# Layer attention with maxima two steps ahead, ends of heads spread over steps, and low parts on VectorE

## The reference

```python
hn = rmsnorm(h, norm_gain[l])
dq, dk, dv, dg, fq, fk, fv, ff, fg = split(hn @ w_in[l])
# differential attention: 4 heads of 2 maps, keys 64 wide, values 128 wide
s = einsum('bhmqd,bhmkd->bhmqk', q, k) * HEAD_DIM ** -0.5      # chunk-wise causal mask
p = softmax(s)
do = einsum('bhqk,bhkd->bhqd', p[:, :, 0] - lam * p[:, :, 1], v)
do = rmsnorm(do, subln_gain[l], 1e-5) * (1.0 - lam_init) * silu(dg)
# forgetting attention: 8 heads, keys and values 64 wide
s = einsum('bhqd,bhkd->bhqk', q, k) * HEAD_DIM ** -0.5 + cq[..., None] - cum_logf[:, :, None, :]
fo = einsum('bhqk,bhkd->bhqd', softmax(s), v) * silu(fg)       # causal mask
h = h + concatenate([do, fo], -1) @ w_out[l]
```

## Time and profile before

| | us |
|---|---|
| median of 3 runs | 1854.41 |
| lowest and highest | 1851.5, 1854.45 |
| the profiled execution | 1854.35 |
| its span | 1852.5 |
| attention of layer 0 | 196 to 331 in the span |
| attention of layer 1 | 551 to 677 in the span |

### The profile page before, as it was taken

One profiled execution on the slowest core, in us unless ns is written; L12 is line 12 of the kernel. 1 busy time (PEld: TensorE's weight loads), 2 busy tenths in 40 slices (PEclk: granted clock), 3 DMA queues, 4 the chain that ended last, 5 costly groups with the idle time before them and its releaser, 6 DMA issues.

```text
span 1852.5 us, 29994 instructions
## 1 busy us (share of the span) xinstructions
PE 1807.5 (98%) x11996; PEld 1630.0 (88%) x11996; DVE 1202.5 (65%) x1687; ACT 815.1 (44%) x1475; POOL 517.5 (28%) x437
## 2 busy tenths in 40 slices
PE   9999999999998899999999999999999999999999
PEld 8999888989988887999988877989877879999887
DVE  7843475575526757999985555646666589999531
ACT  5222466332235754444433324446565554444331
POOL 3443333344342433000034423320133410000343
PEclk9999999999999999999999999999999999999999
DMA  4333120223331112332323223200003223323223
GB/s 167 97 96 109 54 48 24 80 89 101 98 108 42 36 46 91 121 126 96 103 74 98 96 98 126 83 34 1 1 1 114 91 65 118 126 92 103 73 98 103
DMA packets 46170, 154.16 MB, mean 83 GB/s; under 512 B 6096, under 2 KB 6352, under 8 KB 45904
## 3 DMA queue, kind: packets, MB, share of 16 engines
q1 hardware_dynamic: 46032, 152.24, 25.2%
HBM read 140.40 MB, written 2.10 MB: 77 GB/s over the span
## 4 chain that ended last, share of the span: by engine, by line
PE 87%; DVE 7%; ACT 3%; issue 1%; DMA 1%; POOL 0%; SPq 0%; DVEq 0%; ACTq 0%
PE ps L476 23%; PE ps L477 23%; PE ps L478 23%; PE ps L1236 5%; PE ps L1197 4%; PE ps L1218 3%; PE ps L2895 1%; DVE nm L1285 1%; PE ps L2881 1%; PE ps L2864 1%; DVE xl L568 1%; PE ps L2634 1%; PE ps L1437 1%; DMA raw<-wstream 1%; ACT PT L1267 0%
## 5 line engine op out<-in xcount | busy, mean ns | idle before, releaser
L460 POOL TENSOR_TENSOR wl<-raw,wh 128x1024 fp32r<-128x1024 f32 (+1 forms) x166 | 407.2, 2453 | 998.8 <-ACT wh L452 998.8
L452 ACT ACTIVATE wh<-raw 128x1024 fp32r<-128x1024 f32 (+1 forms) x178 | 188.9, 1061 | 547.2 <-PE ps L478 480.8
L476 PE MATMUL ps<-xh,wh 128*128 128x264 f32 (+1 forms) x1120 | 380.0, 339 | 2.6 <-POOL wl L460 1.3
L477 PE MATMUL ps<-xl,wh 128*128 128x264 f32 (+1 forms) x1120 | 375.4, 335 | 0.0
L478 PE MATMUL ps<-xh,wl 128*128 128x264 f32 (+1 forms) x1120 | 374.8, 335 | 0.0
L478 PE MATMUL ps<-XSh,wl 128*128 128x256 f32 (+1 forms) x864 | 283.4, 328 | 0.0
L476 PE MATMUL ps<-XSh,wh 128*128 128x256 f32 (+1 forms) x864 | 283.0, 328 | 0.3 <-DVE wl L1970 0.3
L477 PE MATMUL ps<-XSl,wh 128*128 128x256 f32 (+1 forms) x864 | 283.2, 328 | 0.0
L476 PEld LDWEIGHTS ps<-xh,wh 128*128 128x128 f32 x1120 | 210.5, 188 | 29.6 <-issue 6.9
L477 PEld LDWEIGHTS ps<-xl,wh 128*128 128x128 f32 x1120 | 210.7, 188 | 22.9 <-issue 1.2
L478 PEld LDWEIGHTS ps<-xh,wl 128*128 128x128 f32 x1120 | 210.7, 188 | 22.4
(11 more groups left out here) (451 smaller groups left out, 3648.7 us busy)
## 6 DMA issues: line engine op xcount, KB each, us to landing
raw<-wstream SPq DMA_DIRECT2D x176, 512.0 KB, 3.4
rawx<-wpairs SPq DMA_DIRECT2D x44, 512.0 KB, 3.5
raw<-wpairs SPq DMA_DIRECT2D x24, 512.0 KB, 3.5
raw<-wstream SPq DMA_DIRECT2D x10, 528.0 KB, 3.4
xs<-KA SPq DMA_DIRECT2D x32, 132.0 KB, 2.4
xs<-KB SPq DMA_DIRECT2D x28, 132.0 KB, 2.3
h<-xT SPq DMA_DIRECT2D x4, 528.0 KB, 6.3
out<-h SPq DMA_DIRECT2D x8, 256.0 KB, 4.5
```

Of the source, the lines that this page charges most:

```text
L452: e.activation(wh[p % 2][:, 0:n], raw[c % 2][:, 0:n], ACT.Copy).then_inc(*w_hi(p))
L460: e.tensor_tensor(wl[p % 2][:, 0:n], raw[c % 2][:, 0:n], wh[p % 2][:, 0:n].bitcast(F32), ALU.subtract).then_inc(*w_lo(p))
L476: e.matmul(o, w_h, x_h, start=start, stop=False)
L477: e.matmul(o, w_h, x_l, start=False, stop=False)
```

## The change

It has these parts, all of them in the attention of the two layers, but for the first lines of the last two points:

- On VectorE a unit's maximum is taken at step u-2 if its scores began three steps ahead, else at u-1; the ends of heads come ahead of the maxima within a step.
- Copy and square of a differential head's end are in separate steps. The scaling is folded: in place of a reciprocal and three multiplications by it, one operation makes 128e-5 s0^2 from the sum s0 of the exponentials, which is added to the sum of squares; the copy stays unscaled.
- Ends of fox heads are one step later on VectorE.
- The quads' copies from PSUM go from VectorE to ScalarE.
- The low parts of the heads' outputs go from GpSimd to VectorE, and so do the splits of the first two chunks of `w_out`, now at steps 50 and 54.
- The last values of the meta tokens come first; at step 6 the value block comes ahead of the scores.
- The attention of the meta tokens begins at steps 14 and 25 in place of 26 and 41, in bank 0 in place of 3, and the table of banks and shut stretches follows. The last four heads' tiles are taken in the order 3, 0, 1, 2.
- The first blocks of the output projection stand at steps 61 to 66, in banks 2 and 3.

```diff
-V_SPLIT = {...} | {("wout", l, 2) for l in range(2)}
+V_SPLIT = {...} | {("wout", l, c) for l in range(2) for c in range(3)}
...
-        VALUES_PE = {-2: [(1, 0)], -1: [(2, 0), (0, 0)], 1: [(1, 1)], 2: [(2, 1)], 3: [(0, 1)], 4: [(3, 0)], 5: [(3, 1)],
-                     7: [(4, 0)], 8: [(4, 1)]}
-        VALUES_ACT, VALUES_DVE = {3: (1,), 6: (3,)}, {4: (2, 0), 9: (4,)}
+        VALUES_PE = {-2: [(1, 0)], -1: [(0, 0), (2, 0)], 1: [(0, 1)], 2: [(1, 1)], 3: [(2, 1)], 4: [(3, 0)], 6: [(3, 1)],
+                     8: [(4, 0), (4, 1)]}
+        VALUES_ACT, VALUES_DVE = {3: (1,), 7: (3,)}, {2: (0,), 4: (2,), 9: (4,)}
...
-                            self.items[q], self.on_dve[q] = x.quad[0], True
+                            self.items[q], self.on_dve[q] = x.quad[0], False
... attention_pe
+                if plan.layer is not None and s == 6:
+                    last_values_pe(e, on, plan.layer, s)
                 begin_pe(e, on, plan, s)
-                if plan.layer is not None:
+                if plan.layer is not None and s != 6:
                     last_values_pe(e, on, plan.layer, s)
...
-                if rest and s in (64, 65, 66, 67, 68, 69):
+                if plan.layer is not None and 61 <= s < 67:
                     next(rest)
... attention_dve
-                alone = plan.layer is not None and s + 1 < len(units) and units[s + 1].ahead == 1
-                if s + 1 < len(units) and not alone:
-                    maximum(s + 1)
+                layer = plan.layer is not None
+                if layer:
+                    for key, k in plan.ends.get(s, []):
+                        end_dve(e, on, plan, key, k)
+                for u in (s + 1, s + 2):
+                    if u < len(units) and u - s == (2 if layer and units[u].ahead == 3 and u > 2 else 1):
+                        maximum(u)
...
+                    if s in (50, 54):
+                        split_lo_dve(e, on, PART["wout", plan.layer, s // 4 - 12])
+                else:
+                    for key, k in plan.ends.get(s, []):
+                        end_dve(e, on, plan, key, k)
... attention_pool
-                if s in (49, 53) and plan.layer is not None:
-                    split_lo(e, on, PART["wout", plan.layer, s // 4 - 12])
...
-            return x_lo[("ao",) + key]
+            return (v_lo if key[0] in ("diff", "fox") else x_lo)[("ao",) + key]
... end_dve
             if (kind, k) in (("diff", 6), ("fox", 3)):
-                return
+                return end_low(e, on, key, v_lo)
...
+                if k == 0 and i >= 0:
+                    on.wait_ge(*prob[plan.name, last_unit[key][1]])
+                    s0 = rs[:, i % 2, 0:8:2]
+                    e.scalar_tensor_tensor(q0, s0, 128e-5, s0, ALU.mult, ALU.mult).then_inc(*v_end(*key, "q0"))
+                elif k == 3:
                     on.wait_ge(*a_end[key + ("sq",)])
...
+                    if i >= 0:
+                        on.wait_ge(*v_end.now())
+                        e.tensor_tensor(ms, ms, q0, ALU.add).then_inc(*v_end(*key, "ms"))
... layer_plan
-                shut += [(3, 26, 32), (4, 36, 37), (3, 41, 47), (4, 48, 49)]
+                shut += [(0, 14, 21), (4, 24, 25), (0, 25, 32), (4, 32, 33)]
...
-                for kind, step in (("diff", 26), ("fox", 41)):
+                for kind, step in (("diff", 14), ("fox", 25)):
... wout_begin_pe
-            next_pair(0)
-            claim(on, pair(("wout", l, 0)), wout_shape(l)[2], v_out["wout", l, 0])
-            for k in (0, 1, 2, 4, 5, 6):
-                wout_blocks(e, on, l, 0, (k,))
-                yield k
+            for c, ks in ((0, (0, 1, 2, 4, 5, 6)), (1, (0, 1, 2))):
+                next_pair(2 - 2 * c)
+                claim(on, pair(("wout", l, c)), wout_shape(l)[2], v_out["wout", l, c])
+                for k in ks:
+                    wout_blocks(e, on, l, c, (k,))
+                    yield k
+            next_pair(4)
```

More of the change, by code:

```diff
@@ L71 @@
 PARTS = list(PART)
-V_SPLIT = {(st + part, f) for st in ("ffn1", "ffn2") for part in "gu" for f in range(2, PLAIN)} | {("wout", l, 2) for l in range(2)}
+V_SPLIT = {(st + part, f) for st in ("ffn1", "ffn2") for part in "gu" for f in range(2, PLAIN)} | {("wout", l, c) for l in range(2) for c in range(3)}
 V_SPLIT |= {("ffn2u", 0), ("ffn2g", 1)}
@@ L1112, in __init__ @@
                 self.name, self.units, self.sets, self.PT, self.flip_banks = name, units, sets, PT, flip_banks
-                self.free, self.layer, self.aside = free, layer, set()
+                self.free, self.layer, self.aside, self.rest = free, layer, set(), ()
                 n, nxt = len(units), 0
@@ L1201, in attention_pe @@
             units, name = plan.units, plan.name
-            rest = None
             if plan.layer is not None:
                 last_values_pe(e, on, plan.layer, -2)
-                rest = wout_begin_pe(e, on, plan.layer)
+                plan.rest = rest = wout_begin_pe(e, on, plan.layer)
             begin_pe(e, on, plan, -1)
@@ L1299, in attention_dve @@
                         e.tensor_copy(plan.PT[i % 2][:, 0:n], PS[:, lo:lo + n]).then_inc(*v_flip(name, u))
-                if alone:
-                    maximum(s + 1)
-                if plan.layer is not None:
+                if layer:
                     last_values_dve(e, on, plan.layer, s)
@@ L1319, in attention_dve @@
                             key_low_dve(e, on, plan.layer, *head)
-                for key, k in plan.ends.get(s, []):
-                    end_dve(e, on, plan, key, k)
+                    if s in (50, 54):
[3 more added lines that the diff above has]
+                        end_dve(e, on, plan, key, k)
         def meta_values_pool(e, on, l):
@@ L1447, in end_act @@
                 compressed_act(e, on, key[1], k)
-            elif key[0] == "diff" and k == 0:
+            elif key[0] == "diff" and k in (1, 2):
                 _, _, i, nq, _ = head_shape(key)
@@ L1456, in end_act @@
                 to = fin[0:nq, f, 0:512]
-                if before:
-                    on.wait_ge(*x_hi[("ao",) + before])
-                    on.wait_ge(*ao_lo(before))
-                e.activation(to, src, ACT.Copy).then_inc(*a_end(*key, "copy"))
+                if k == 1:
+                    if before:
+                        on.wait_ge(*x_hi[("ao",) + before])
+                        on.wait_ge(*ao_lo(before))
+                    e.activation(to, src, ACT.Copy).then_inc(*a_end(*key, "copy"))
+                    return
                 on.wait_ge(*a_end[key + ("copy",)])
                 e.activation(osb[0:nq, f, 0:512], to, ACT.Square).then_inc(*a_end(*key, "sq"))
-            elif key[0] == "diff" and k == 2:
+            elif key[0] == "diff" and k == 3:
                 _, _, i, nq, _ = head_shape(key)
@@ L1534, in end_dve @@
                 d, o = osb[0:nq, f, 0:w], PS[0:nq, 512 * b:512 * b + w]
+                k -= kind == "fox"
                 if k == 0:
@@ L1574, in end_pool @@
                     end_pool(e, on, plan, (key[1], key[2], -1), k - 5)
-            elif (key[0], k) in (("mem", 2), ("nsa1", 5), ("diff", 6), ("fox", 3)):
+            elif (key[0], k) in (("mem", 2), ("nsa1", 5)):
                 end_low(e, on, key, x_lo)
@@ L1688, in layer_plan @@
             if l == 0:
-                ends[3:3], ends[6:6] = [("diff", -1)], [("fox", -1)]
+                ends[1:1], ends[4:4] = [("diff", -1)], [("fox", -1)]
             for kind, i in ends:
@@ L1694, in layer_plan @@
             heads = [[("fox", c, i, q) for i in two_] for c in range(4) for q in range(2)
-                     for two_ in ((0, 1), (2, 3))]
+                     for two_ in (((3, 0), (1, 2)) if c == 3 and q else ((0, 1), (2, 3)))]
             pairs = maps[:4] + heads[:2] + [x for pair_ in zip(maps[4:], heads[2:-2]) for x in pair_] + heads[-2:]
@@ L1771, in wout_blocks @@
             on.wait_ge(*w_hi[p])
[L1772 removed]
+            on.wait_ge(*low_part(p))
             for k in ks:
@@ L1792, in wout_pe @@
             end_pe(e, on, plans[l], *plans[l].held)
-            claim(on, pair(("wout", l, 1)), halves, v_out["wout", l, 1])
-            wout_blocks(e, on, l, 1, (0, 1, 2))
+            for _ in plans[l].rest:
+                pass
             wout_blocks(e, on, l, 0, (3, 7), True).then_inc(*tile("wout", l, 0))
@@ L3242, in gpsimd @@
                 attention_pool(e, on, plans[l])
-                parts_pool(e, on, ("wout", l, 1), ("wout", l, 7))
+                for q in range(PART["wout", l, 3], PART["wout", l, 7] + 3):
+                    split_lo(e, on, q)
             ffn_pool(e, on, "ffn1")
```

29 lines of the change are left out of this document (9 added, 20 removed).

## The result

The changed kernel takes 1860.29 us (median of 13 runs, 1857.41 to 1863.34), the kernel before beside it 1855.68. The ratio is 1.0023, 95% interval 1.0012 to 1.0034: the change makes it slower by 4.3 us (the two medians differ by 4.6), where 11.5 faster was forecast. The profiled execution took 1860.29, its span is 1858.5.

What follows compares the result with a forecast made beforehand. TensorE was taken as the bound, with time to win only in its 22.8 us idle over both attentions and its half-clock stretches. Gains 16.3 less costs 4.8 made 11.5 us: 1854.4 to 1843, range 1834 to 1854.

Steps and rivals of the forecast that it cites:

- (a): Start of both attentions: meta tokens' last value block first, its copy earlier, so TensorE's wait for it goes; gain 2.6 us.
- (d): GpSimd's subtractions (low parts, first weight splits) leave the attentions, so VectorE's small operations aren't stretched; gain 1.8 us.
- (e): Meta tokens' attention moves to steps 14 and 25: waits of 2.9 us go, 1.0 charged at fox head 0; gain 1.9.
- (b): Step 6: a value block ahead of the scores covers their wait for a key head's low part; gain 1.2 us.
- (c): Ends of differential heads: copy and square in successive steps, so transposed copies behind them aren't late; gain 3.6 us.
- (f): Two of three half-clock stretches in the attentions go with the waits ahead of them; gain 3.1 us.
- (g): Maxima two steps ahead spare a third of the remaining 6.3 us of waits for the transposed copy; gain 2.1 us.
- (j): VectorE takes low parts and splits, gives up quads' copies; net load mostly beside TensorE; cost 1.8 us, bounds 0 and 16.
- the slower rival: VectorE becomes the bound: low parts and splits ahead of maxima reach TensorE; +10 us, 1864; chance 0.1.
- (h): End of each attention: earlier output blocks leave the last scaling and transpose uncovered, about 0.9 us a layer; cost 1.8.
- The last rival: VectorE's subtractions hold GpSimd's small copies for the quads: 6 us, 1849; given part of another rival's chance of 0.15.
- (i): Quads' copies on ScalarE stand between exponentials in both attentions; cost 1.2 us, bounds 0 and 11.

Runs made afterwards that it cites:

- low_behind: The changed kernel with the heads' low parts still on VectorE, but behind the maxima and mix of their step: 1855.05 us, ratio to before 1.0006.
- square_with_copy: The changed kernel with the square of a differential head's output directly behind its copy, the sum left in place: 1860.61 us, ratio to before 1.0022.
- meta_last: The fastest kernel: tail_pool_square with the meta tokens' small VectorE operations behind the heads' ends of the same step; 1849.04 us, ratio to before 0.9959.
- near_maxima: The changed kernel with every maximum taken one step ahead: ratio to before 1.0028.
- tail_pool_square: The changed kernel with first output column at steps 64 to 69, heads' low parts on GpSimd, square behind the copy: 1852.25 us, ratio to before 0.9980.
- tail_late: The changed kernel with the six blocks of the first output column at steps 64 to 69 again: 1855.58 us, ratio to before 1.0016.
- splits_pool: meta_last with the low parts of the first two chunks of output weights on GpSimd again, at steps 49 and 53: 1850.19 us, ratio to before 0.9966.
- low_pool: The changed kernel with the heads' low parts on GpSimd again, the weight splits staying on VectorE: 1854.55 us, ratio to before 1.0001.

## Why the prediction was wrong

Of the gains, (a), (d) and (e) were read right; (b), (c) and (f) didn't come, nor did (g) in the changed kernel. Of the costs, the worst was said to be hidden. The forecast's own sign of being wrong nearly came: of the 10.5 us of waits for the transposed copy 9.4 are left.

(j) failed, and it is the step on which the sign turned. It said that what is queued behind a low part "is a maximum or a mix of two maps, waited for two steps later". But the change moves the ends ahead of the maxima, and where a score is only one or two steps ahead, its maximum is waited for at once: low part, maximum, exponential, copy, transpose are one chain. 1.8 us were charged with the splits; the low parts alone measure 0.22%, 4.1 us (4.6 at like clock), and 3.3 of it comes back when they only move behind the maxima (`low_behind`). Part (j) also priced the wrong thing. It put VectorE's load at a net of some 8 us more, but VectorE's busy time in the attentions fell: the 32 one-column products alone, which GpSimd's subtractions had held, took 12.8 us before and take 7.1 now. My evidence was averages, 79 of 121 us; the slower rival had the mechanism, at a price that assumed every low part on the path.

(c) failed. The waits of the earlier trace rows did go; that the chain behind them starts later while its transpose stays was not followed. Forecast +3.6; in the changed kernel waits of 1.27 and 1.87 stand in the place of 1.01 and 1.00. What a good placing is worth is seen in part in `square_with_copy` (1.3 at like clock) and `meta_last` (1.5); no run puts copy and square back where they stood, so the size of (c) as a whole is read from waits and not measured.

(f) didn't come. In the two profiled executions it went the other way, 6.8 us more at half clock where 10.2 less were forecast. Over all executions the clock is the same: a mean of 0.9952 in the changed kernel's 13, and 0.9954 in 112 of the kernel before; so the change gives no clock back, and its loss isn't the clock's either (3.8 of it stands at like clock). That a stretch belongs to the wait beside it is not shown: TensorE has the same wait of 1.87 or 1.88 at differential head 0 of layer 0 in four kernels, and within 2 us of its end a stretch of 10.24 begins in the changed kernel, one of 3.41 in `near_maxima` and in `low_behind`, and none in `tail_pool_square`, nor anywhere else in its layer 0.

(h): 0.85 with the low parts on GpSimd is the forecast's 0.9. With them on VectorE it is 1.8 a layer; it was an interaction of (h) and (j) that the sum had not. The whole of the early blocks measures 4.3 us at like clock (`tail_late`), where (h) charged 1.8; that is within its bound of 2.5 a layer.

(e) was right in what it gains and had the collision in the wrong place: not fox head 0 but differential head 0. In the fastest kernel the early place is worth 0.25%, 4.6 us, against 1.9 and (f)'s share, and 2.2 at like clock; in the changed kernel the collision takes a part back, and 1.3 is left.

(a) was right: 1.6 us a layer against 1.3. (b) is nothing, by its wait: at step 6 the key head's low part is still 0.6 late, as far behind the block as before.

(d) was right as a mechanism. The rule of the Trainium skill (SBUF — State Buffer, "Who interferes with whom") that it rested on is borne out by two runs, 2.74 us against 0.69 (`splits_pool`) and 946 ns against 244 (`low_pool`). Its size for the splits is 1.1 us by the milestones and 1.7 at like clock, against 1.8. For the heads' low parts leaving GpSimd was no gain: the stretched operation there had slack. The last rival, the same lock in the other direction, is there too (the last section has its rows), but in neither attention does TensorE wait for GpSimd, so it cost nothing that the profile shows.

(g): 2.1 forecast; nothing in the changed kernel, 1.8 ± 1.0 at like clock in the fastest. The pair of steps 20-21 is still there, as said (1.22 at 591.38 in layer 1, 1.22 before). (i): a cost of 1.2 forecast, none found; taking the edit back gives -0.4 ± 0.8 in the changed kernel and +1.0 ± 1.1 in the fastest.

Still open is what the new order of tiles does (it is that of the last fox head's four tiles, of no other head): a wait of 0.83 or more at step 60, which the kernel before doesn't have, is in all kernels with the changed banks. It was not tried alone. Nor were the ends' place ahead of the maxima as a whole, the fox ends' later step and the folded scaling; what they gain or cost is not known.

## What to carry to other kernels

Ask of each operation that is moved what stands behind it in its engine's order and when that is due; an engine with a third of its time free still delays a chain that passes through it. When the start of a chain is moved a step later, look at the step in which its last member is consumed. Put the operations that feed the nearest deadline first: four small edits of place, order and engine took the same work from 1860 to 1849 us. And where executions differ in clock by more than kernels do in time, compare the kernels at like clock before a ratio is called undecided.

## What the hardware showed that I had not expected

A 512-column VectorE product was held for the whole of a GpSimd subtraction of 1024 columns (2.74 in place of 0.69), though only small operations, of one and four columns, were held in the trace before. It goes both ways. In the changed kernel GpSimd's copy of 16 columns takes 0.20 us alone, but 0.60 beside VectorE's low parts and 1.13 beside its weight split, and ends with them:

```profile
641.39 1.22 DVE L472 TENSOR_TENSOR wl<-raw,wh 128x1024 fp32r<-128x1024 f32 x1
```

```profile
641.54 1.13 POOL L1374 COPY LF<-Pb 128x16 f32<-128x16 f32 x1 [0.37 <-DVE Pb L1318]
642.61 0.19 POOL L1374 COPY PMf<-Pb 128x16 f32<-128x16 f32 x1
```

And the clock differs between executions of one kernel about as much as between kernels: the same wait of TensorE, 1.87 or 1.88 us, had 10.24 us at half clock beside it, 3.41, or none. The halved stretches of two profiled executions, 20.5 us in the changed kernel and 6.8 in `meta_last`, overstate the difference; by the mean clock of all executions it is 18 against 13 us at half clock over the whole span (13 and 6 executions).
